# Small TensorE products of a mixer padded to the full array, score blocks cut to 32 columns

## The reference

```
retention:  scores = (q @ k.T) * decay_mask          # decay depends on the distance alone
            o = scores @ v + (q * q_decay) @ S
            S = S * chunk_decay + (k * k_decay).T @ v
GLA:        log_a = log_sigmoid(a_lr @ w_gla_a2 + b_gla_a) / 16
            A[i, j] = sum_d q[i, d] * k[j, d] * exp(cum[i, d] - cum[j, d])   for j <= i
            o = A @ v + (q * exp(cum)) @ S
            S = S * exp(cum_last) + (k * exp(cum_last - cum)).T @ v
```

## Time and profile before

| | |
|---|---|
| median of 3 runs | 3632.55 us |
| profiled execution, span | 3629.5 us |
| TensorE (PE) busy in the span | 3497.8 us, 96% |
| VectorE (DVE) busy | 2569.0 us, 71% |
| ScalarE (ACT) busy | 1318.8 us, 36% |
| mixer stage on PE | 204.6 us to 853 us |

### The profile page before, as it was taken

One profiled execution on the slowest core, in us unless ns is written; L12 is line 12 of the kernel. 1 busy time (PEld: TensorE's weight loads), 2 busy tenths in 40 slices (PEclk: granted clock), 3 DMA queues, 4 the chain that ended last, 5 costly groups with the idle time before them and its releaser, 6 DMA issues. The chain is left out here.

```text
span 3629.5 us, 45839 instructions
## 1 busy us (share of the span) xinstructions
PE 3497.8 (96%) x17879; PEld 3058.5 (84%) x17879; DVE 2569.0 (71%) x3799; ACT 1318.8 (36%) x1675; POOL 973.0 (27%) x619
## 2 busy tenths in 40 slices
PE   8999999998998999999999999999899999999997
PEld 6877777777876889999999999999788888888885
DVE  4135555553324138999998888886789999899997
ACT  5111133542223123332326776774222222222223
POOL 0000000000000000133333434342456655555552
PEclk9999999999999999999999999999999999999998
DMA  5145333435424234688889999999999999999996
GB/s 203 53 136 173 118 121 127 137 111 197 151 93 172 95 144 152 234 331 319 306 323 347 380 384 378 388 384 357 351 388 360 381 384 355 380 359 375 380 354 250
DMA packets 193653, 964.92 MB, mean 266 GB/s; under 512 B 19697, under 2 KB 67121, under 8 KB 92706
## 3 DMA queue, kind: packets, MB, share of 16 engines
q1 hardware_dynamic: 116034, 464.59, 35.0%
q0 software_dynamic: 61424, 426.27, 30.1%
q10 hardware_dynamic: 15984, 71.17, 5.0%
HBM read 865.58 MB, written 96.37 MB: 265 GB/s over the span
## 5 line engine op out<-in xcount | busy, mean ns | idle before, releaser
L2070 PE MATMUL hidden_hp<-dense_hi,whi 128*128 128x384 f32 x2048 | 697.7, 341 | 6.1 <-PEq L123 6.1
L2071 PE MATMUL hidden_hp<-dense_lo,whi 128*128 128x384 f32 x2048 | 689.3, 337 | 0.0
L1845 ACT CAST whi<-raw 128x2048 fp32r<-128x2048 f32 x214 | 411.7, 1924 | 752.7 <-PE outputs_vp L2628 470.7
L2017 POOL DMA_INDIRECT hidden_row<-u_rows,expert_ids x192 | 381.8, 1989 | 975.6 <-DVE dots L2302 597.9
L2621 PE MATMUL outputs_vp<-whi,outputs_w_hi 128*128 128x512 f32 x1536 | 598.9, 390 | 15.1 <-DVE outputs_w_lo L2521 13.0
L2622 PE MATMUL outputs_vp<-whi,outputs_w_lo 128*128 128x512 f32 x1536 | 598.4, 390 | 0.0
L1849 DVE TENSOR_TENSOR wlo<-raw,whi 128x2048 fp32r<-128x2048 f32 x214 | 490.5, 2292 | 98.8 <-ACT whi L1845 97.8
L2357 POOL DMA_INDIRECT outputs_row<-v_rows,outputs_id x192 | 378.9, 1973 | 476.1 <-DVE accg L2546 407.6
L2302 DVE CUSTOM_DVE_ANT_0 hidden_row<-hidden_row,hidden_h_row 128x2048 f32<-128x2048 f32 x192 | 436.2, 2288 | 64.9 <-DMA hidden_row<-u_rows,expert_ids 64.1
L2546 DVE SCALAR_TENSOR_TENSOR accg<-outputs_row,outputs_w_op,accg 128x2048 f32<-128x2048 f32 x192 | 450.9, 2348 | 35.2 <-DMA outputs_row<-v_rows,outputs_id 29.4
L2070 PEld LDWEIGHTS hidden_hp<-dense_hi,whi 128*128 128x128 f32 x2048 | 386.2, 189 | 6.5 <-issue 6.5
(11 more groups left out here) (384 smaller groups left out, 4923.5 us busy)
## 6 DMA issues: line engine op xcount, KB each, us to landing
raw<-v_units SPq DMA_DIRECT2D x128, 1024.0 KB
raw<-u_units SPq DMA_DIRECT2D x86, 1024.0 KB
raw<-w_in SPq DMA_DIRECT2D x42, 1024.0 KB, 6.0
hidden_raw<-u_units SPq DMA_DIRECT2D x42, 1024.0 KB
hidden<-hidden_hid SPq DMA_DIRECT2D x128, 192.0 KB
gate_mat<-units_big SPq DMA_DIRECT2D x12, 2048.0 KB, 20.9
units_big<-hidden ACTq DMA_DIRECT2D x15, 1536.0 KB
units_big<-gate_mat ACTq DMA_DIRECT2D x15, 1536.0 KB
```

The source lines that it names most:

```text
L1845: self.nc.scalar.copy(self.hi[s][:], self.raw[raw][:]).then_inc(self.hi_done, 1)
L2017: pool.indirect_dma_start(row[g % U_ROWS][:], None, u_rows, bass.IndirectOffsetOnAxis(expert_ids[:, g:g + 1], 0)).then_inc(row_in[g % U_RO ...
L2070: mm(o, un.hi[s][:, x, :], h_hi[:, x, :], start=x == 0, stop=False)
L2071: mm(o, un.hi[s][:, x, :], h_lo[:, x, :], start=False, stop=False)
```

## The change

Every tile that a small product reads is made 128 rows high, and cleared once at the start, so that these products run 128 rows deep with 128 stationary columns. `out_head` and `scores_r` take 128 stationary columns of which the upper 64 carry nothing; `turn` transposes all 128 rows. In `scores_g` the loops over the 8-query pieces s and the blocks g change places, so that consecutive products write to different 32-column groups; the blocks ahead of the diagonal become six products of 32 columns per head in place of three of 32, 64 and 96, and come after all pieces of that head. VectorE clears six tiles more.

```diff
-        v_s = a.sb("v_s", [NSMP, 2, DV])
+        v_s = a.sb("v_s", [P, 2, DV])
-        at, at_s = a.sb("at", [P, 2, P]), a.sb("at_s", [NSMP, 2, NSMP])
+        at, at_s = a.sb("at", [P, 2, P]), a.sb("at_s", [P, 3, NSMP])
-        km = a.sb("km", [NSMP, NSEQ, DK])
+        km = a.sb("km", [P, NSEQ, DK])
-        wa2 = a.sb("wa2", [RANK + 1, H * DK])
-        alr = a.sb("alr", [RANK + 1, SEQ + NSMP])
+        wa2 = a.sb("wa2", [P, H * DK])
+        alr = a.sb("alr", [P, SEQ + NSMP])
-        sc, zo = X[:, 0:2 * P], X[0:NSMP, 2 * P:4 * P]
+        sc, zo = X[:, 0:2 * P], X[:, 2 * P:4 * P]
+        def kl_columns(t, h):
+
+            at_ = seg(t, None) - 2 * rows(t) + h * rows(t)
+            return dec[:, at_:at_ + P]
...
-            sp.wait_ge(ones_set, 1)
+            sp.wait_ge(ones_set, 2)
...
-                nc.scalar.copy(qkT[:, :, 0:R], T[:, :, 0:R]).then_inc(t_used, 1)
+                nc.scalar.copy(qkT[:], T[:]).then_inc(t_used, 1)
...
-                tt(km[:], bcast(kd_s[:, h, :], 1, NSEQ), bcast(seq_rows[:], 2, DK), mult).then_inc(k_masked, 1)
+                tt(km[0:NSMP], bcast(kd_s[:, h, :], 1, NSEQ), bcast(seq_rows[:], 2, DK), mult).then_inc(k_masked, 1)
...
-            nc.vector.memset(qm[:], 0.0).then_inc(zeros_set, 1)
-            vec.wait_ge(zeros_set, 1)
+            nc.vector.memset(wa2[:], 0.0).then_inc(ones_set, 1)
+            for x in (qm[:], km[NSMP:P], v_s[NSMP:P], at_s[:], qk[NSMP:P], dec[:]):
+                nc.vector.memset(x, 0.0).then_inc(zeros_set, 1)
+            vec.wait_ge(zeros_set, 6)
...
-                    ins = nc.tensor.transpose(T[:, x, 0:R], src[0:R, x, :], ident[0:R, 0:R])
+                    ins = nc.tensor.transpose(T[:, x, :], src[:, x, :], ident[:])
...
-                    ins = mm(sc[0:R, h * R:(h + 1) * R], qkT[:, 2 + h, 0:R], qkT[:, h, 0:R], start=True, stop=True)
+                    ins = mm(sc[:, h * R:(h + 1) * R], qkT[:, 2 + h, :], qkT[:, h, 0:R], start=True, stop=True)
...
                 for h in range(2):
-                    for g in range(R // BLK):
-                        for s in range(BLK // SUB):
+                    for s in range(BLK // SUB):
+                        for g in range(R // BLK):
                             at_ = BLK * g + SUB * s
                             ins = mm(sc[BLK * g:BLK * (g + 1), h * R + at_:h * R + at_ + SUB], D[:, h, g, s, :],
                                      h3(seg(t, "Q8"))[:, h, at_:at_ + SUB], start=True, stop=True)
-                        if g > 0 and not smp:
-                            ins = mm(sc[0:BLK * g, h * R + BLK * g:h * R + BLK * (g + 1)], h3(seg(t, f"O{g}"))[:, h, :],
-                                     h3(seg(t, "QO"))[:, h, BLK * (g - 1):BLK * g], start=True, stop=True)
+                    for g, b in () if smp else ((1, 0), (2, 1), (3, 2), (2, 0), (3, 1), (3, 0)):
+                        rows_, cols = slice(BLK * b, BLK * (b + 1)), slice(h * R + BLK * g, h * R + BLK * (g + 1))
+                        ins = mm(sc[rows_, cols], h3(seg(t, f"O{g}"))[:, h, rows_],
+                                 h3(seg(t, "QO"))[:, h, BLK * (g - 1):BLK * g], start=True, stop=True)
...
-                    ins = nc.tensor.transpose(T[0:R, h, :], h3(seg(t, "KL"))[:, h, :], ident[:])
+                    ins = nc.tensor.transpose(T[:, h, :], kl_columns(t, h), ident[:])
...
-                mm(zo, at_s[:, h, :], v_s[:, h, :], start=True, stop=False)
+                mm(zo, at_s[:, h:h + 2, :], v_s[:, h, :], start=True, stop=False)
...
-                    ins = mm(zo, qm[:, NSMP * b:NSMP * (b + 1)], S8[k % 2][:, b, :], start=False, stop=b == NSEQ - 1)
+                    ins = mm(zo, qm[:, NSMP * b:NSMP * b + P], S8[k % 2][:, b, :], start=False, stop=b == NSEQ - 1)
```

More of the change, by code:

```diff
@@ L750, in project_and_mix @@
                       (seq_rows[:], c["seq_rows"]), (kdec[:], c["kdec"]), (qdec[:], c["qdec"]), (mask_r[:], c["mask_r"])]
-        gla_consts = [(wa2[:], w_a2), (alr[0:RANK, :], alr_dram), (keep_s[:], c["keep_s"][:, 0:2 * NSMP]),
+        gla_consts = [(wa2[0:RANK + 1, :], w_a2), (alr[0:RANK, :], alr_dram), (keep_s[:], c["keep_s"][:, 0:2 * NSMP]),
                       (keep[:], c["keep"][:, 0:2 * P]), (causal_s[:], c["causal_s"]), (causal[:], c["causal"])]
@@ L923, in load_v_s @@
                 v_landed(g)
-                sp.dma_start(v_s[:].rearrange("p h d -> p (h d)"), proj[SEQ:SEQ + NSMP, at_:at_ + COLS]).then_inc(vs_in, 16)
+                sp.dma_start(v_s[0:NSMP].rearrange("p h d -> p (h d)"), proj[SEQ:SEQ + NSMP, at_:at_ + COLS]).then_inc(vs_in, 16)
             def load_norm(g):
@@ L1098, in copy_qk @@
             def copy_qk(m):
-                R = rows(tile_of(m))
                 act.wait_ge(t_made, t_at["turn", m] + 1)
@@ L1110, in copy_head @@
                 wait(act, s_stored, 16 * (k // 2))
-                nc.scalar.copy(out_s[:, DV * (k % 2):DV * (k % 2 + 1)], zo).then_inc(x_used, 1)
+                nc.scalar.copy(out_s[:, DV * (k % 2):DV * (k % 2 + 1)], zo[0:NSMP, :]).then_inc(x_used, 1)
             def log_of_z(m):
@@ L1289, in mask_r_scores @@
                     vec.wait_ge(o_made, nth(m))
-                to, by = (at_s, mask_rs) if t == SMP else (at, mask_r)
-                tt(to[:], h3(sc[0:R, 0:2 * R]), by[:, h0:h0 + 2, :], mult).then_inc(x_used, 1)
+                to, by = (at_s[0:R, 0:2, :], mask_rs) if t == SMP else (at[:], mask_r)
+                tt(to, h3(sc[0:R, 0:2 * R]), by[:, h0:h0 + 2, :], mult).then_inc(x_used, 1)
             def step_state(m, decay):
@@ L1396, in mask_g_scores @@
                 if m == INST // 2:
-                    vec.wait_ge(zeros_set, 3)
+                    vec.wait_ge(zeros_set, 8)
                 scv = h3(sc[0:R, 0:2 * R])
-                to, msk = (at_s, causal_s) if smp else (at, causal)
+                to, msk = (at_s[:, 0:2, :], causal_s) if smp else (at, causal)
                 for g in range(R // BLK):
@@ L1613, in turn @@
             def turn(m):
-                t = tile_of(m)
-                R, src = rows(t), rot if is_ret(m) else qk
+                src = rot if is_ret(m) else qk
                 if is_ret(m):
```

## The result

The changed kernel takes 3591.8 us (median of 4 runs, 3588.62 to 3598.56), the kernel before 3633.6 on the same chip; the ratio is 0.9884, 95% interval 0.987 to 0.9898: 42 us less. The forecast was 3590. The profiled execution spans 3586.5 us, 43.0 less than before, and its own run took 3588.62, so what lies around the span is 2.1 us.

What follows compares the result with a forecast made beforehand. The prediction took PE, busy 96% of the span, as the bound; 21.2 + 14.0 + 8.6 - 1.0 = 42.8 us off 3629.5 gave 3586.7, and 3.1 for the median made it 3590 us, range 3580 to 3614.

Steps and rivals of the forecast that it cites:

- Padding: Small products in the mixer stage padded to 128 lose their shape-change borders: 21.2 us saved, bounds 18 and 24.
- the rest: Sample-tile turns, retention score groups and sample score passes also lose borders but get wider operands: 1.0 us saved.
- about 0.2 each: PE empties itself when the array's shape changes, once going into a small group and once out: about 0.2 us each.
- Score passes: Eight GLA score passes of prompt tiles fall from 3.32 to 1.57 us each: 14.0 us saved, bounds -4 and 15.
- The issue: Rival: a GLA pass's 88 records go no faster than 39 ns each; about 3616 us, chance 0.10.
- column-group rivals: Rival: in GLA passes a change of column group costs as a change of shape does; 3660 us, chance 0.03.
- Borders stay: Rival: the 0.39 us per state group stays with padding, only the passes get shorter; about 3610 us, chance 0.07.
- Clock: Half-clock time of PE in the mixer stage, mostly behind score passes, partly goes: 8.6 us saved, bounds 0 and 12.
- Held back: PE's savings ahead of waits set by VectorE and ScalarE are lost: 1.0 us in all.
- Cover: VectorE's added clears, 4.8 us, fit into its 11.7 us wait for the constants right behind.
- Around the span: For the whole kernel, the median time was taken to lie 3.1 us above the profiled span.
- likeliest case: The whole kernel if the forecast itself holds: 3580 to 3602 us, chance 0.75.

Runs made afterwards that it cites:

- padding alone: The changed kernel with the score loops of the kernel before: 3616.6 us, ratio 0.9959.
- the heads: The changed kernel with the products of a sample head back at 64 stationary columns, depth 128 kept: 3594.7 us, ratio 0.9896.
- states-twice kernel: The kernel before with each state product of the samples issued twice: 3656.9 us, ratio 1.0067.
- scores alone: The kernel before with only the new body of `scores_g`: 3612.4 us, ratio 0.9943.

## Why the prediction was right

*Padding.* Forecast 21.2 us: states 12.5, heads 3.7, gates 4.0, the rest 1.0. Measured, from the same groups: 32 x 0.39 = 12.5, 8 x 0.49 = 3.9, the ten gate pairs together 3.6 (most 0.38 or 0.39); the rest gave 0.9 (two sample passes 0.17 each, two retention score groups 0.13, two sample turns 0.15; the other two sample turns mostly wait for others). 20.9 us. The 0.17 of a sample pass is no border, though: with padding alone that pass takes 0.03 us more than before, with the new score loops alone 0.20 less. That the 0.39 stands at the borders was argued from two starts; the states issued twice show it, and the heads show it for the width. The starts of single records bear out "about 0.2 each" too: against the group of the earlier trace rows, that of the earlier trace rows loses 0.09 us ahead of its first record and 0.10 behind it, none between its middle ones, and 0.20 from its last record to the second projection product.

*Score passes.* Forecast 1.57 us each, 14.0 in all; measured 1.38, 15.5 in all. The step was the pace of the 88 records: I took 12.5 ns from four starts in the old trace, it is 10. The issue and the column-group rivals are gone by this row alone: neighbours in different groups start about 7 ns apart. "Borders stay" is gone by the state group's 1.78 us.

*Clock.* Forecast 8.6 us back; measured 27.3 to 10.2 us of half clock, 8.5 if half of it is lost. The number is near and its reason only half right: I took each fall behind a pass as caused by the pass. The same passes in two other kernels were followed by one only 3 times out of 12; what came back was one draw, and with the draw of the states-twice kernel it would have been nothing. That it came near the forecast is in part luck. The three stretches that remained are the ones that the forecast left, each at a wait.

*Held back.* Forecast 1.0. The terms above add up to 20.9 + 15.5 + 8.5 = 44.9 and the stage lost 42.2, so 2.7 us went. The two timelines laid beside each other, start by start, show most of it. About 1.1 is the clock: against the same groups at full clock, the 27.3 us of half clock cost 12.4 us and the 10.2 us cost 5.0, so 7.4 came back and not 8.5. Small products lose less than half: in the earlier trace rows's stretch the pieces of one column group start 53 ns apart in place of 32. Another 1.0 went into waits, as forecast, because PE arrives earlier: the two before the passes grew from 4.2 to 4.6 us in all, and a head's wait from 0.3 to 0.7, by which this head lost all of its 0.49. The total of the waits hides it (9.1 before, 9.0 after), as the one of 1.0 at the stage's start, for VectorE's rotated queries and keys, is down to 0.1. That one is no gain: the clock at the start was half for 2.1 us longer, PE came to the wait about 0.9 us later, and the turn behind it began at the same time. The last 0.6 us I can't place.

*Cover.* The six clears take 4.6 us (forecast 4.8) and end at 211.6 us; VectorE then still waits 5.9 us, until 217.5. The stage's start didn't move (first transposes at 220.1 us before and at 220.0 after).

*Around the span.* I used 3.1 us, the profiled run shows 2.1.

*Sums that were off.* None of them enters the 42.8. At 62 ns a record the passes would have lost about 21 us, not 17. A change of column group would have had to cost about 0.12 us, not 0.06, to eat the padding's gain (a pass 2.65 us longer than 3.32, less 0.47, over 44 changes). The low end of the likeliest case adds up to 3582 and not 3580. And that the four starts in the earlier trace rows belong to three column groups stands in no row; it was taken from the order of the loops.

## What to carry over

Between full-shape products on PE, a small group of another depth or width cost 0.33 to 0.49 us more than the same group at full shape, once per group, whether it held two products or four; where the operands can be kept clear at no cost, give it the full shape. Where the full shape also made the stationary tile or the transpose of a product with 64 moving columns wider (retention scores and turns of sample tiles), only 0.13 and 0.15 us came back. Where products must be narrow, give all of them one width and let neighbours write different column groups: that took a pass from 2.87 to 0.88 us with 16% more records. Credit a clock that was seen to fall in one trace only as a chance, and look for it in a second trace.

## What the runs showed of the hardware that was not expected

- Neighbouring records in four column groups start about 7 ns apart, 88 of them in 0.88 us; eight-column records in one group start 32 ns apart. The Trainium skill, "TensorE: Matmul & The Clock Gate", section "Wait — 56ns, not 53.3ns?", gives about 25 ns as the least distance; the trace agrees for one group and not across groups.
- The three wide products of a head (32, 64, 96 columns) cost 0.67 us with their changes of shape, the six narrow ones in their place about 0.19 us (534.32 to 534.51 in the changed kernel's pass).
- The half clock behind the same 2.9 us pass came in 6 of 18 cases.
- The later stages, with the same code, differed by up to 11 us between profiled executions. The longest, with scores alone, had 95 us of half clock in them and before had 87, which is some 4 of the 10 us between these two; the rest is open.
